# Embedding products behind the attention, replanned row products and gathers in a two-layer attention, recurrence and product-key expert kernel

## The reference, cut to what matters

```python
mix = hybrid_mixer(h, w_in[i], fox_fb[i], fox_norm_g[i], lower_bounds[i], hg_norm_g[i], w_out[i])
h = layer_norm(DEEPNORM_ALPHA * h + mix, ln1_g[i], ln1_b[i])
ffn = peer_ffn(h, peer_wq[i], peer_keys[i], peer_u[i], peer_v[i])
ple = jax.nn.sigmoid(h @ ple_gate_w[i]) * (p[i] @ ple_w[i])
h = layer_norm(DEEPNORM_ALPHA * h + ffn + ple, ln2_g[i], ln2_b[i])
```

```python
act = jax.nn.gelu(jnp.einsum('thkd,td->thk', u[idx], xb).astype(jnp.float32), approximate=False)
return jnp.einsum('thk,thkd->td', (gate * act).astype(xb.dtype), v[idx])
```

## Time and profile before

| what | us |
|---|---|
| median of 3 runs (3529.05 to 3531.75) | 3529.09 |
| the profiled execution | 3543.67 |
| its span, first to last instruction | 3541.7 |
| TensorE busy | 3320.1 (94%) |
| VectorE busy | 2519.8 (71%) |
| POOL busy | 2078.6 (59%) |
| ScalarE busy | 1376.0 (39%) |

### The profile page before, as it was taken

The page is one execution under the profiler, slowest core; times in us unless marked ns, Lnnn a source line. Parts: engine busy times, 40 slices in busy tenths (PEclk is TensorE's granted clock), DMA queues, the critical chain, the costliest instruction groups (busy, mean ns, idle before and its releaser), DMA issues. The chain is left out here.

```text
span 3541.7 us, 47011 instructions
## 1 busy us (share of the span) xinstructions
PE 3320.1 (94%) x17370; PEld 2933.3 (83%) x17370; DVE 2519.8 (71%) x4637; ACT 1376.0 (39%) x2682; POOL 2078.6 (59%) x1388
## 2 busy tenths in 40 slices
PE   5997799999999999999889977999999999999996
PEld 5776687999999977888777766879999999788885
DVE  5945339987864478888866633699778544888888
ACT  1234012366666533333212420124666664333332
POOL 5920575776666665555479025767766666555552
PEclk9999899999999999999999988999999999999998
DMA  3210222878887999999622012248888889999994
GB/s 120 92 36 19 72 95 101 281 286 307 295 293 293 325 356 365 356 355 354 245 82 88 11 42 72 84 169 268 291 296 302 301 301 336 348 358 352 353 356 170
DMA packets 312675, 817.11 MB, mean 231 GB/s; under 512 B 22272, under 2 KB 119552, under 8 KB 309120
## 3 DMA queue, kind: packets, MB, share of 16 engines
q1 hardware_dynamic: 112256, 349.02, 28.3%
q0 software_dynamic: 73728, 268.47, 20.0%
q10 hardware_dynamic: 126464, 196.63, 16.1%
HBM read 712.84 MB, written 101.19 MB: 230 GB/s over the span
## 5 line engine op out<-in xcount | busy, mean ns | idle before, releaser
L1206 POOL TENSOR_TENSOR u_lo<-panel,u_hi 128x1024 fp32r<-128x1024 f32 x256 | 617.3, 2412 | 318.7 <-ACT u_hi L1022 317.8
L576 PE MATMUL ps<-hT_hi,u_lo 128*128 128x384 f32 x2048 | 702.8, 343 | 6.2 <-POOL u_lo L1206 6.2
L576 PE MATMUL ps<-hT_lo,u_hi 128*128 128x384 f32 x2048 | 685.6, 335 | 0.0
L576 PE MATMUL ps<-hT_hi,u_hi 128*128 128x384 f32 x2048 | 685.5, 335 | 0.0
L576 PE MATMUL ps<-v_hi,w_lo 128*128 128x512 f32 x1536 | 601.1, 391 | 17.9 <-DVE w_lo L1721 17.5
L576 PE MATMUL ps<-v_lo,w_hi 128*128 128x512 f32 x1536 | 600.3, 391 | 0.0
L576 PE MATMUL ps<-v_hi,w_hi 128*128 128x512 f32 x1536 | 600.1, 391 | 0.0
L1159 POOL TENSOR_TENSOR ring_hi<-panel,cst 128x512 fp32r<-128x512 f32 x244 | 275.1, 1128 | 539.3 <-PE ps L559 307.1
L1221 POOL TENSOR_TENSOR v_lo<-panel,v_hi 128x1024 fp32r<-128x1024 f32 x128 | 317.6, 2481 | 394.8 <-ACT v_hi L1071 394.7
L1071 ACT CAST v_hi<-panel 128x1024 fp32r<-128x1024 f32 x256 | 269.0, 1051 | 629.0 <-PE ps L576 588.8
L1643 DVE TENSOR_TENSOR arena<-ps,arena 128x512 f32<-128x512 f32 x384 | 247.0, 685 | 292.0 <-PE ps L830 292.0
(11 more groups left out here) (249 smaller groups left out, 5802.1 us busy)
## 6 DMA issues: line engine op xcount, KB each, us to landing
panel<-in_u SPq DMA_DIRECT2D x256, 512.0 KB, 4.3
panel<-in_v SPq DMA_DIRECT2D x256, 512.0 KB, 6.9
gate_scratch<-arena ACTq DMA_DIRECT2D x24, 2048.0 KB, 9.2
act_scratch<-arena ACTq DMA_DIRECT2D x124, 384.0 KB, 3.5
arena<-act_scratch ACTq DMA_DIRECT2D x62, 768.0 KB, 6.5
arena<-gate_scratch ACTq DMA_DIRECT2D x62, 768.0 KB, 13.6
panel<-in_w_in SPq DMA_DIRECT2D x28, 1024.0 KB, 5.2
panel<-in_wq SPq DMA_DIRECT2D x16, 1024.0 KB, 5.1
```

The costliest lines, as they stand in the source:

```text
L576: mm = nc.tensor.matmul(o, lhs[a], rhs[b_], start=(start and n == 0), stop=(stop and n == 2))
L1206: pr.mark(nc.gpsimd.tensor_tensor(u_lo[:, j % URING].rearrange("p c n -> p (c n)"), u_tile(j), u_hi[:, j % URING].rearrange("p c n -> p (c ...
```

## The change

It does five things. (1) The embedding products leave the gate stage. TensorE makes them right after the last attention step and before `turn(mix)`, into eight PSUM banks that are free then (`PLE_BANKS`); ScalarE copies them to spare places in SBUF (`ple_part`, `ple_keep`), four before and four after `root(2)`. Their operands are loaded by SP into rows of `rows_mem` after the first attention score; the panel `K_PLE` is gone, and the expert tiles change their two slots of `panel`. (2) The two halves of the gate product follow each other. VectorE takes embedding values from SBUF and adds tiles 0 to 3 in routing parts 7 and 8, and 4 to 7 in parts 13 to 16. (3) `split_u(0)` and `split_u(1)` stand between the gate halves in ScalarE's list, and the first `u` tiles are loaded one weight panel earlier. (4) The one-hot steps begin two tiles later (`FIRST_CHUNK` 26). Only 2 row products and half of the key steps of block 2 stand before them; the rest of the keys are in one-hot steps 0 to 4, routing parts of block 2 in steps 6 to 19, one a step, where they were in every second step; from step 58 on every second step has two row products (`DOTS`). (5) POOL issues its first gather at tile 11 (`FIRST_GATHER`), and each later one when `DOTS` says that its buffer is free.

The diff, cut to its core:

```diff
-FIRST_CHUNK = 24
+FIRST_CHUNK = 26
 TURNS = {FIRST_CHUNK - 4: 1, FIRST_CHUNK + 28: 2, FIRST_CHUNK + 60: 3}
-EARLY_DOTS = 18
+EARLY_DOTS = 2
 LATE_DOTS = 6
+DOTS = [EARLY_DOTS]
+for chunk_ in range(NK - FIRST_CHUNK):
+    DOTS.append(min(DOTS[-1] + 1 + (chunk_ >= 58 and chunk_ % 2 == 0), SLOTS - LATE_DOTS))
+FIRST_GATHER = 11
...
+PLE_BANKS = (1, 2, 0, 5, 3, 6, 4, 7)
...
+        ple_rows = rows_mem[:, 5:7, :]
+        pT_rows = rows_mem[:, 7, :].rearrange("p (c t) -> p c t", t=T)
...
+        ple_part = [work[:, 1088:1600], state[:].rearrange("p h d -> p (h d)"), part(8192, 512), pTs[:, 0, :],
+                    pTs[:, 1, :], part(11648, 512), ng[:, 0, :], ng[:, 1, :]]
...
-            return panel[:, j % 4 // 2, j % 2 * D:(j % 2 + 1) * D]
+            return panel[:, 1 - j % 4 // 2, j % 2 * D:(j % 2 + 1) * D]
...
+                        sp.wait_ge(scored.sem, layer * scored.per_layer + 1)
+                        pr.mark(sp.dma_start(ple_rows, ple_w[at].rearrange("l (c p) n -> p (l c) n", p=P)), ple_in, 16)
+                        pr.mark(sp.dma_start(pT_rows, pT[at].rearrange("l (c p) t -> p (l c) t", p=P)), ple_in, 16)
                         sp.wait_ge(a_done.sem, layer * a_done.per_layer + NH)
                         for n, a in enumerate((ln1_g, ln1_b)):
                             pr.mark(sp.dma_start(lng[:, n, :], row(a)), ln1_in, 16)
-                        pr.mark(sp.dma_start(pTs[:], pT[at].rearrange("l (c p) t -> p (l c) t", p=P)), pT_in, 16)
...
-                    if j < 2:
-                        sp.wait_ge(ring_lo_ready.sem, layer * ring_lo_ready.per_layer + SPLITS)
-                    elif j < TILE_SLOTS:
-                        sp.wait_ge(pled.sem, layer * pled.per_layer + 8)
+                    if j < TILE_SLOTS:
+                        sp.wait_ge(ring_lo_ready.sem, layer * ring_lo_ready.per_layer + SPLITS - (KC if j < 2 else 0))
...
+                PLE_FREED = [at_ready, at_ready, probs_ready, probs_ready, state_ready, probsT_ready, o_out, fox_out]
+                pe.wait_ge(ple_in.sem, layer * ple_in.per_layer + 32)
+                for g in range(8):
+                    half, i = g // 4, g % 4
+                    done = PLE_FREED[g]
+                    pe.wait_ge(done.sem, (layer + 1) * done.per_layer)
+                    for c in range(2):
+                        mm = nc.tensor.matmul(ps[:, PLE_BANKS[g], :], pT_rows[:, c, i * P:(i + 1) * P],
+                                              ple_rows[:, c, half * 512:(half + 1) * 512], start=(c == 0), stop=(c == 1))
+                    pr.mark(mm, pled)
                 pe.wait_ge(mix_ready.sem, layer * mix_ready.per_layer + 2)
+                pe.wait_ge(ple_kept.sem, layer * ple_kept.per_layer + 8)
...
-                    project([take6(8 * half + i, (gate_sig, 4 * half + i + 1)) for i in range(NT)], True)
-                    if half == 0:
-                        pe.wait_ge(pT_in.sem, layer * pT_in.per_layer + 16)
-                        pe.wait_ge(panel_in[K_PLE % 2].sem,
-                                   layer * panel_in[K_PLE % 2].per_layer + 16 * (K_PLE // 2 + 1))
-                    for i in range(NT):
-                        o = take6(8 * half + 4 + i, (ple_mul, 4 * half + i + 1))
-                        for c in range(2):
-                            mm = nc.tensor.matmul(o, pTs[:, c, i * P:(i + 1) * P],
-                                                  wp[:, c, half * 512:(half + 1) * 512], start=(c == 0), stop=(c == 1))
-                        pr.mark(mm, pled)
+                    project([take6(4 * half + i, (gate_sig, 4 * half + i + 1)) for i in range(NT)], True)
...
-                        pe.wait_ge(gate_sig.sem, layer * gate_sig.per_layer + 7 + j)
-                    elif j == 2:
-                        pe.wait_ge(ple_mul.sem, layer * ple_mul.per_layer + 5)
+                    if j < 3:
+                        pe.wait_ge(gate_sig.sem, layer * gate_sig.per_layer + 5 + j)
...
+                def ple_keep(g):
+                    act.wait_ge(pled.sem, layer * pled.per_layer + g + 1)
+                    if g == 6:
+                        act.wait_ge(mix_ready.sem, layer * mix_ready.per_layer + 1)
+                    if g == 7:
+                        act.wait_ge(gains_read.sem, layer * gains_read.per_layer + 1)
+                    pr.mark(nc.scalar.copy(ple_part[g], ps[:, PLE_BANKS[g], :]), ple_kept)
                 root(1, fox_ssq[:])
+                for g in range(4):
+                    ple_keep(g)
...
                 root(2, ssq[:])
+                for g in range(4, 8):
+                    ple_keep(g)
...
+                    if g == 4:
+                        split_u(0)
+                        split_u(1)
...
-                EXPONENTIALS = {10: 1, FIRST_CHUNK + 8: 2, FIRST_CHUNK + 51: 3}
-                for j in range(URING):
+                EXPONENTIALS = {14: 1, FIRST_CHUNK + 11: 2, FIRST_CHUNK + 51: 3}
...
-                    if j == 3:
+                    if j == FIRST_GATHER:
                         pool.wait_ge(acc_init.sem, layer * acc_init.per_layer + 8)
                         pool.wait_ge(idx_ready.sem, layer * idx_ready.per_layer + 1)
-                    if j >= 3:
-                        gather_u(j - 3)
-                for s in range(NK - 3, SLOTS - 1):
+                    while sent < min(j + 1 - FIRST_GATHER if sent < UBUF else SLOTS, UBUF + (DOTS[j - 1 - FIRST_CHUNK] if j > FIRST_CHUNK else 0),
+                                     SLOTS - 1):
+                        gather_u(sent)
+                        sent += 1
...
-                step(last)
+                pr.mark(last, gains_read)
+                dve.wait_ge(gains_read.sem, layer * gains_read.per_layer + 1)
...
-                    dve.wait_ge(pled.sem, layer * pled.per_layer + g + 1)
-                    pr.mark(nc.vector.tensor_tensor(gg, gg, ps[:, (8 * half + 4 + i) % 6, :], ALU.mult), ple_mul)
+                    dve.wait_ge(ple_kept.sem, layer * ple_kept.per_layer + g + 1)
+                    pr.mark(nc.vector.tensor_tensor(gg, gg, ple_part[g], ALU.mult), ple_mul)
...
-                    if 9 <= k < 13:
+                    if k in (7, 8):
+                        for g in range(2 * k - 14, 2 * k - 12):
+                            ple(g)
+                    if 13 <= k < 17:
                         ple(k - 9)
-                    if k == 16:
-                        for g in range(4, 8):
-                            ple(g)
                 for part_ in range(5):
                     key_tops(1, 3, part_)
                 for k in range(5, 19):
                     routing(1, k)
-                    if k >= 7:
-                        dot(k - 7)
-                for q in range(NT):
+                for q in range(2):
                     for part_ in range(5):
                         key_tops(2, q, part_)
-                        if part_ == 4 and 12 + q < EARLY_DOTS:
-                            dot(12 + q)
-                for s in range(16, EARLY_DOTS):
+                for s in range(EARLY_DOTS):
                     dot(s)
                 dve.wait_ge(iota_ready.sem, layer * iota_ready.per_layer + 1)
                 for k in range(NG):
                     one_hots(k)
-                    if k % 2 == 0 and k // 2 < 14:
-                        routing(2, 5 + k // 2)
+                    if k < 5:
+                        for part_ in (2 * k, 2 * k + 1):
+                            key_tops(2, 2 + part_ // 5, part_ % 5)
+                    if 6 <= k < 20:
+                        routing(2, k - 1)
                     if 27 <= k < 47:
                         key_tops(3, (k - 27) // 5, (k - 27) % 5)
                     if 46 <= k < 60:
                         routing(3, k - 41)
-                    if EARLY_DOTS + k < SLOTS:
-                        dot(EARLY_DOTS + k)
-                for s in range(EARLY_DOTS + NG, SLOTS - LATE_DOTS):
+                    for s in range(DOTS[k], DOTS[k + 1]):
+                        dot(s)
+                for s in range(DOTS[NG], SLOTS - LATE_DOTS):
```

40 lines of the change are left out of this document (19 added, 21 removed).

## The result

The change made the kernel faster by 32 us, not by 61: the median is 3497.7 us (3495.3 to 3499.4, 4 runs) against 3530.1 us (3529.1 to 3531.8, 4 runs), a ratio of 0.9903 (0.9890 to 0.9917). The sign was right; the time lies 29.5 us above the forecast of 3468.2 and outside the range.

What follows compares the result with a forecast made beforehand. TensorE was taken as the bound, so only its standstills counted: 45.8 + 12.5 + 2.6 = 60.9 us off the median of 3529.1 gave 3468.2 us, range 3459 to 3486.

Steps and rivals of the forecast that it cites:

- Term A: Gate stage: with the halves joined, TensorE starts expert tiles 22.9 us earlier a layer; 45.8 us off.
- term C: Attention end: embedding products fill TensorE's idle time and the transposes run warm; 1.3 us a layer, 2.6 us off.
- Term B: Before the one-hots: waits for u_lo and one-hot rows and the clock drop go, little comes back; 12.5 us off.
- rival 1: Routing steps of block 2: VectorE takes 1 us more in each of eight; 17.2 us lost, 3485 us; chance 10%.
- The value stage: TensorE's waits for w_lo before the value tiles, 17.5 us, stay unchanged despite later gate writes.
- rival 2: Joined gate stage: POOL cannot get ahead, u_lo comes late, up to 5.6 us a layer, 3479 us; chance 7%.
- rival 3: Attention end: embedding products run cold at clock 0.50, 15.3 us a layer lost, 3499 us; chance 5%.
- rival 5: One-hot steps: all fourteen routing steps take 10.5 us, 69.6 us a layer come back, 3606 us, slower; chance 3%.

Runs made afterwards that it cites:

- the plan alone: New plan of row products, keys, gathers and exponentials put into the kernel before, embedding products left in the old gate stage: 3518.4 us, ratio 0.9961.
- second profile of before: The kernel before, unchanged, run again for another profile: 3533.1 us, ratio 0.9997.
- POOL quiet: Changed kernel with exponentials of block 1 at tile 18 instead of 14, POOL subtracting only 128 of 1024 columns in tiles 3 to 21: 3464.8 us.
- tile 18: Changed kernel with ScalarE's exponentials of block 1 at tile 18 instead of 14: 3495.1 us, ratio 0.9891.
- Two halves of a change: Changed kernel with the old plan put back: 3538.1 us; kernel before with only the new plan: 3518.4 us.
- the three edits together: Changed kernel with exponentials of block 1 at tile 18, first one-hot step at tile 28, compares of block 1 against PSUM: 3490.2 us, ratio 0.9871.

## Why the prediction was wrong, step by step

**Term A, gate stage joined (45.8), and term C, end of the attention (2.6): right.** Together 24.2 us a layer were forecast. The u tiles begin 598.2 - 574.6 = 23.6 us earlier in the first layer (from profile to profile this start moves by up to 5 us, nearly all of it ahead of the attention's end; from the first transpose to the first `u_lo` matmul it is 252.4 us before and 228.4 after, 24.0 less); in the second, counted from the start of the last value matmul before (1756.9 and 1740.1), 585.1 - 561.3 = 23.8. The forecast rows came out nearly to the digit: transposes 3.71 us (3.7 forecast), root at 339.04 (339.3 to 339.5), no gap at the first tile.

**Term B, "before the one-hots" (12.5 off): the step that failed.** It said that VectorE gives up 21 us, nearly what TensorE gains, that two tiles more add room, "so the waits go". The u stage grew by 6.1 us a layer instead of falling by 6.25: 24.7 of the 29.5 us by which the forecast missed (1.0 more is in terms A and C, 2.6 in the `w_lo` waits). The first half of the step was sound, as the plan alone shows (8.3 us a layer off). What failed is the silent assumption that VectorE's other instructions keep their durations of before; and the step looked only at the first one-hot rows, not at the table, which TensorE wants four tiles earlier. The eight embedding products now read SBUF beside POOL and take 14.2 us (4.6 + 3.2 + 2.9 + 1.8 + 1.7) instead of 5.5; the sixteen compares and sixteen multiplications of 800 numbers in the stretch from 540 to 690 us take 52.6 (28.4 + 24.2) instead of 37.3 (20.0 + 17.3, second profile of before); the additions into `h` behind the embedding products (L1658) take 10.0 instead of 7.5. That is 26.5 us, and the table was 26.4 us later than reckoned (682.8 for 656.4); smaller shifts nearly cancel. Two causes show in the rows. The plan alone makes 5.5 of the 15.3 us in compares and multiplications, since it takes away the row products that held POOL's subtractions off them (the step of before shown with the plan alone). The rest comes with the joined stages: before, part of block 0's routing fell into pauses of POOL, while it waited for TensorE (17.27 us in the earlier trace rows) and for ScalarE; now it falls beside a nearly unbroken row of subtractions.

I had weighed the Trainium skill ("SBUF — State Buffer", section "SBUF: two separate sides") there: a VectorE instruction with two SBUF inputs and a GpSimd instruction that reads SBUF lock each other out for a whole instruction. The rows agree: with two SBUF operands 0.98 us without POOL and 2.0 or more beside it, with one operand in PSUM, or in the reduction, 0.98 beside POOL too. I named the eight embedding products and all routing steps, but priced the hold only by rival 1, for the one-hot loop and the routing of block 2, and not in front of it, where most of the two-SBUF work stands and where a whole block's table hangs on it.

**Rival 1, "VectorE slips in the routing steps": the right mechanism, but elsewhere.** Its 3485 was nearer to the time than the forecast, but that is luck: its place was not where the changed kernel lost. I put 1 us more on each of eight steps; in the lock it is 1.35 (2.34 for 0.99), and 29 us in all instead of 17. In the changed kernel itself the steps run at 5.4 us, as forecast, and the one-hot wait is gone. What I did not see is that it is decided by VectorE's lead at the first step, 4.3 us here, and by what releases POOL's gathers: 3.7 us of lead less tip it over, and where a gather does not wait for the row product of its own step the same small lead does no harm (3496.4 us).

**The value stage: near.** Unchanged was forecast. Against the second profile of before, whose `w_lo` waits are 10.2 us, the changed kernel has 12.8. My 17.5 came from one profile that was 14.6 us above its median.

**Rivals 2, 3 and 5** did not occur: POOL kept its lead, the products ran at clock 1.00, and no routing step was near 7.7 us in the changed kernel.

No run separates the embedding products from the routing. The trace with POOL quiet gives their shares against tile 18, as far as POOL was quiet: 14.7 us in the compares and multiplications and 4.4 in the embedding products; the rest is spread over smaller instructions.

## What to carry to other kernels

When an engine is brought forward, read again the durations of the engine that feeds it under the neighbours it will now have; a price from a stretch where the neighbour paused is not the price beside it. Two halves of a change can each be worth little (+5 and -15 us) and 32 us together, so ask which list is late next after both. Work taken out of a list can also take away an order that kept two engines off each other, as the row products did here. A list in which one engine waits for a result of the same step of another can fall into a slow rhythm that holds itself: release it by the result of the step before.

## What the runs showed of the hardware

A VectorE instruction with both operands in SBUF, asked for 0.89 us into a POOL subtraction of 2.37 us, took 2.34 instead of 0.99. The time is in the recorded duration of the instruction, no view of waits shows it; over the 107 us between the first expert matmul and the table of block 1 it made at least 28 us.

A wait of TensorE costs more than itself. Behind the wait of 6.07 us at tile 22 the clock stood at 0.50 for another 4.51 us (last row of the stretches above), which is 2.3 us more. Behind the wait of 4.67 us at tile 16 it stood there for 3.12 us, behind the one of 11.8 us with tile 18 for some 4 us. So two waits of 4.7 and 6.1 us cost 10.8 + 3.8 = 14.6 us, one of 11.8 us about 13.9, and the u stages differ by 0.8 us; cutting the one wait in two other pieces gained nothing.

The lock can set in or not in one and the same kernel: with the three edits together the runs lay between 3480.6 and 3502.8 us, and the profiled one, the slowest, had it in its second layer only, whose u stage was 9.1 us longer than the first's (635.7 and 626.6). Whether the faster runs had it is not shown, since they have no profile, and part of the slowest run's length lies elsewhere.
